# Kept merge weights, a ring that grows from 10 to 12 slots, later output sums and early norms in a streaming encoder with gathered experts

## What is computed

```python
def layer(x, ...):
    h = rmsnorm(x, norm1_g)
    z = h @ w_in                      # three mixers' inputs and three gates per channel
    ...                               # A: gated linear recurrence, B: pooling, C: differential attention
    g = sigmoid(gates).reshape(B, T, 3, D_MODEL)
    m = g[:, :, 0] * (ya @ proj_a) + g[:, :, 1] * (yb @ proj_b) + g[:, :, 2] * (yc @ proj_c)
    x = x + m @ w_out
    x = x + peer(rmsnorm(x, norm2_g), peer_wq, peer_subkeys, peer_u, peer_v)

def peer(h, wq, subkeys, u, v):
    q = (h @ wq).reshape(n, 8, 2, 128)
    s = einsum('nhpd,pkd->nhpk', q, subkeys)
    top_s, top_i = top_k(s, 16)                       # per half of the key
    best_s, best_c = top_k(all sums of the two halves, 16)
    idx, gate = i1 * 128 + i2, softmax(best_s)        # 8 heads x 16 experts for each token
    act = gelu(einsum('nd,nhkd->nhk', h, u[idx]))
    return einsum('nhk,nhkd->nd', gate * act, v[idx])
```

## Time and profile before

| | us |
|---|---|
| median of 3 runs (2737.83 to 2743.10) | 2740.68 |
| the profiled execution | 2747.89 |
| its span in the profile | 2746.2 |
| layer 0: mixers, experts | 24 to 407, 407 to 1374 |
| layer 1: mixers, experts | 1390 to 1767, 1767 to 2728 |

### The profile page before, as it was taken

One profiled execution on the slowest core, in us unless ns is written; L12 is line 12 of the kernel. 1 busy time (PEld: TensorE's weight loads), 2 busy tenths in 40 slices (PEclk: granted clock), 3 DMA queues, 4 the chain that ended last, 5 costly groups with the idle time before them and its releaser, 6 DMA issues.

```text
span 2746.2 us, 37846 instructions
## 1 busy us (share of the span) xinstructions
PE 2055.8 (75%) x11668; PEld 1180.6 (43%) x11668; DVE 1591.9 (58%) x4244; ACT 699.0 (25%) x1688; POOL 776.8 (28%) x831
## 2 busy tenths in 40 slices
PE   6999988887777665555689999888877775665555
PEld 4566776664343211111256667756643441111111
DVE  2544236564667777777535341455646677777774
ACT  3422213331312222112233221133313132212112
POOL 0122003332343344443201220132313434334431
PEclk9999999998898788888899999999988988788887
DMA  6134559998899999999842347599989999999996
GB/s 198 33 96 154 206 199 418 417 418 345 352 420 411 391 390 389 385 397 387 326 121 60 95 146 259 215 417 417 418 326 370 416 407 375 391 393 387 393 389 241
DMA packets 209345, 862.93 MB, mean 314 GB/s; under 512 B 20144, under 2 KB 91328, under 8 KB 127232
## 3 DMA queue, kind: packets, MB, share of 16 engines
q0 software_dynamic: 95280, 677.21, 60.7%
q1 hardware_dynamic: 113872, 183.38, 19.0%
HBM read 853.82 MB, written 6.71 MB: 313 GB/s over the span
## 4 chain that ended last, share of the span: by engine, by line
DMA 28%; PE 28%; DVE 13%; issue 12%; PEldq 7%; PEld 4%; DVEq 3%; ACT 2%; POOL 2%; ACTq 0%; POOLq 0%; SPq 0%
DMA MIX_RINGS<-in_peer_uv_dram,IDX 23%; PE ps L699 9%; PEldq L922 7%; PE ps L936 4%; DVE MIX_RINGS L1474 3%; DMA W<-in_peer_uv_dram,IDX 3%; PE ps L711 3%; DVEq L1322 3%; PE ps L789 2%; PEld ps L920 2%; PE ps L920 2%; PEld ps L761 2%; PE ps L745 1%; PE ps L727 1%; ACT GC L1131 1%
## 5 line engine op out<-in xcount | busy, mean ns | idle before, releaser
L920 PE MATMUL ps<-MIX_RINGS,GC 64*64 64x512 f32 x4272 | 685.0, 713 | 337.9 <-ACT GC L1131 298.2
L646 POOL DMA_INDIRECT MIX_RINGS<-in_peer_uv_dram,IDX x448 | 484.8, 1082 | 1019.6 <-PEq L922 657.7
L920 PEld LDWEIGHTS ps<-MIX_RINGS,GC 64*64 64x64 f32 x4272 | 199.3, 156 | 701.4 <-issue 701.2
L1474 DVE CUSTOM_DVE_ANT_0 MIX_RINGS<-MIX_RINGS 128x1024 f32<-128x1024 f32 x270 | 324.5, 1224 | 139.5 <-DMA MIX_RINGS<-in_peer_uv_dram,IDX 129.7
L1131 ACT ACTIVATE GC<-twins,WV 128x64 f32<-128x64 f32 x640 | 170.7, 336 | 637.2 <-DVEq L1487 636.6
L1474 DVE CUSTOM_DVE_ANT_0 MIX_RINGS<-MIX_RINGS,WQKV_E 128x1024 f32<-128x1024 f32 x178 | 215.0, 1225 | 152.8 <-DMA MIX_RINGS<-in_peer_uv_dram,IDX 146.0
L920 PE MATMUL ps<-W,GC 64*64 64x512 f32 x1248 | 180.5, 708 | 108.2 <-ACT GC L1131 93.8
L699 PE MATMUL ps<-WQKV_E,HT 128*128 128x384 f32 x768 | 252.8, 486 | 0.7 <-issue 0.7
L920 PE MATMUL ps<-WQKV_E,GC 64*64 64x512 f32 x624 | 151.6, 706 | 98.9 <-ACT GC L1131 85.2
L1126 ACT ACTIVATE GV<-AV 128x4 f32<-128x4 f32 x160 | 32.9, 205 | 703.7 <-DVEq L1475 703.6
L646 POOL DMA_INDIRECT W<-in_peer_uv_dram,IDX x128 | 136.3, 1065 | 242.4 <-PEq L922 214.9
(11 more groups left out here) (255 smaller groups left out, 2808.0 us busy)
## 6 DMA issues: line engine op xcount, KB each, us to landing
W<-in_merge_w_dram SPq DMA_DIRECT2D x40, 1024.0 KB, 4.9
W<-in_merge_w_dram SPq DMA_DIRECT2D x80, 512.0 KB, 9.6
WQKV_E<-in_w_in_dram SPq DMA_DIRECT2D x48, 512.0 KB, 6.6
W<-in_out_w_dram SPq DMA_DIRECT2D x16, 1024.0 KB, 10.5
W<-in_query_w_dram SPq DMA_DIRECT2D x16, 1024.0 KB, 11.2
W<-in_w_in_dram SPq DMA_DIRECT2D x12, 1024.0 KB, 8.2
W<-in_query_w_dram SPq DMA_DIRECT2D x20, 512.0 KB, 10.6
MIX_RINGS<-in_peer_uv_dram,IDX POOLq DMA_INDIRECT x448, 11.1
```

The source lines that it names most:

```text
L646: pool.indirect_dma_start(UV[p % RING], None, table, bass.IndirectOffsetOnAxis(IDX[:, n % 2, j:j + 1], 0))\
L920: pe.matmul(ps[o:o + CHUNK, n:n + 512], w[r, :], v[r, d * 512:(d + 1) * 512], start=False, stop=False, skip_group_check=True)
L1474: dve.tensor_tensor_reduce(u, u, HN[t], 1.0, 0.0, ALU.mult, ALU.add, AV[:, j:j + 1])
```

## The change

The change has these parts:

- **Kept weights.** `KEPT = 2`: the weights of the last merge unit of tile 0 (column blocks 6 and 7) stay in W and serve the chunks 0 to 3, `BLOCK_OF` maps chunks to column blocks. `out_w` for `first_output` goes to four other areas (`OUTW`) and the chunks 4 to 15 load their halves, 30 instead of 40. A chunk's weights are issued behind the query half of the step.
- **Ring.** `JOIN` gives the pick from which a slot takes part. There are ten slots from the first pick, of which the last two (W[2], W[4]) wait until chunk 3 is done, and two more: W[3] from pick 84 (step 21), W[1] from pick 160 (step 40). Each pick takes the slot used longest ago.
- **Output sums.** DVE adds output sum u in step u + 16 instead of u + 15. Norm 2 of tiles 1 and 2 moves from step 19 to 20, the rest queries from 21 to 22. The route of unit 8 is spread differently over the parts, and the clearing for tile 2 comes one step later.
- **Early norms.** All gain rows come in one tensor `gains`. The first is loaded right behind the input, that of the next layer (or the final one) within the expert phase. Norm 1 of the next layer for tile 0 is computed by DVE in step 35, for tile 1 in step 79 between dots and weigh; PE turns tile 0 at step 78 and tile 1 behind the last step. At the boundary only tile 2 is left. Only unit 0 of `w_in` is loaded before the boundary, and units 1 to 5 behind the small loads (`FF_SLOT`).
- **Order on PE.** chunk(s+3) goes ahead of experts(s). The gates of chunk 0 go ahead of the turn of norm 2 for tile 0. On DVE the clearing of tile 0's sums goes behind the first route.

```diff
+JOIN = [0] * 10 + [84, 160]
+SLOT_OF, PREV, NTH = [], [], []
+for _p in range(PICKS):
+    _last = [max([q for q in range(_p) if SLOT_OF[q] == r], default=r - len(JOIN)) if JOIN[r] <= _p else PICKS
+             for r in range(len(JOIN))]
+    _r = _last.index(min(_last))
...
-FF_SLOT = (2, 0, 1, 3, 4, 2)
+FF_SLOT = (0, 2, 3, 4, 1, 0)
...
+KEPT = 2
+BLOCK_OF = [KC - KEPT + i if i < KEPT else i - KEPT for i in range(KC)]
...
-Q_STEP = OUT_STEP + GB + 3
+TURN_STEP = OUT_STEP + GB + 2
+Q_STEP = TURN_STEP + 2
...
-        WH = [W2[i // 2][:, i % 2] for i in range(6)]
+        WH = [W2[i][:, k] for i in (0, 1, 3) for k in range(2)]
...
-        UV = [MIX[:, i, :] for i in range(1, 5)] + [W[:, i].rearrange("p c n -> p (c n)") for i in (3, 4)]\
-            + [UVX] + [MIX[:, i, :] for i in (5, 6, 7)]
+        WF = [W[:, i].rearrange("p c n -> p (c n)") for i in range(SLOTS)]
+        UV = [MIX[:, i, :] for i in range(1, 5)] + [UVX] + [MIX[:, i, :] for i in (5, 6, 7)] + [WF[i] for i in (2, 4, 3, 1)]
+        OUTW = [two(x).rearrange("p k (c n) -> p k c n", c=KC) for x in (MIX[:, 1, :], MIX[:, 2, :], UVX, MIX[:, 0, :])]
...
+            sp.dma_start(G, bcast(gains[0])).then_inc(gain_in.sem, 16)
             sp.wait_ge(setup.sem, 8)
...
-                for u in range(3):
-                    ff_unit(u)
-
+                ff_unit(0)
                 sp.wait_ge(*layer_done.at(l, 0))
-                sp.dma_start(G, bcast(norm1_g[l])).then_inc(gain_in.sem, 16)
...
-                for u in range(3, 3 * HB):
+                for u in range(1, 3 * HB):
                     ff_unit(u)
...
                 def chunk_weights(c):
+                    dc = c // 2
                     for i in CHUNK_W[c % 2]:
-                        if c < 2:
-                            sp.wait_ge(*w_used[i // 2].at(l, BEFORE_REST[i // 2]))
+                        if dc == KEPT:
+                            sp.wait_ge(*half_used[(0, 0, 1, 1, 3)[i]].at(l, 1 + (0, 1, 0, 1, 0)[i]))
                         else:
-                            sp.wait_ge(*half_used[i].at(l, c // 2))
+                            sp.wait_ge(*half_used[i].at(l, dc))
...
-                for c in range(AHEAD):
-                    chunk_weights(c)
                 for s in range(4 * (PH - AHEAD)):
-                    if s + AHEAD < CHUNKS:
-                        chunk_weights(s + AHEAD)
                     if s % 4 < 2:
                         query_half(s // 4 * 2 + s % 4)
+                    if 2 * KEPT <= s + AHEAD + 1 < CHUNKS:
+                        chunk_weights(s + AHEAD + 1)
...
+                sp.wait_ge(*gain_used.at(l, 2))
                 sp.nop(nofuse=True)
-            sp.wait_ge(*layer_done.at(DEPTH, 0))
-            sp.dma_start(G, bcast(final_g)).then_inc(gain_in.sem, 16)
+                sp.dma_start(G, gains[bass.ds(l * 2 + 2, 1)].rearrange("a d -> (a d)").partition_broadcast(P))\
+                    .then_inc(gain_in.sem, 16)
...
-                    if RING - AHEAD <= p < RING:
-                        pool.wait_ge(*pq_ps.at(l, p - (RING - AHEAD) + 1))
-                    pool.wait_ge(*uv_free.at(l, p + 1 - RING))
+                    r = SLOT_OF[p]
+                    if NTH[p] == 0:
+                        if r in (5, 6, 7):
+                            pool.wait_ge(*pq_ps.at(l, r - 4))
+                        if r in (8, 9):
+                            pool.wait_ge(*cb_ps.at(l, 2 * KEPT))
+                        if r == 10:
+                            pool.wait_ge(*half_used[4].at(l, KC))
+                            pool.nop(nofuse=True)
+                            pool.wait_ge(*wqh_used.at(l, 2 * (PH - AHEAD)))
+                        if r == 11:
+                            pool.wait_ge(*w_used[1].at(l, SLOT_USES[1]))
+                    else:
+                        pool.wait_ge(*uv_free.at(l, PREV[p] + 1))
...
+            norm_turn(0, 0, range(2))
             with pe.Fori(0, DEPTH) as l:
-                norm_turn(l, 0, range(TILES))
+                norm_turn(l, 0, [2])
...
+                chunk(l, 0, [0])
                 norm_turn(l, 1, [0])
...
-                chunk(l, 0)
+                chunk(l, 0, [1])
...
-                    experts(l, s)
                     if s + AHEAD < CHUNKS:
                         chunk(l, s + AHEAD)
+                    experts(l, s)
...
-                    if s == OUT_STEP + GB + 1:
+                    if s == TURN_STEP:
                         norm_turn(l, 1, [1, 2])
...
+                    if s == GROUPS - 2:
+                        pe.wait_ge(*x_done.at(l, 2))
+                        norm_turn(l + 1, 0, [0])
+                norm_turn(l + 1, 0, [1])
...
+                    if s == GROUPS - 1:
+                        turned(l + 1, 0, range(2))
...
-                clear(0)
                 route(l, 0, range(4))
+                dve.wait_ge(*nt_ev.at(l, (TILES + 1) * TURNS))
+                dve.nop(nofuse=True)
+                clear(0)
...
-                    if 0 <= s - OUT_STEP - 1 < GB:
-                        rest_output(l, s - OUT_STEP - 1)
-                    if s == OUT_STEP + GB + 1:
+                    if 0 <= s - OUT_STEP - 2 < GB:
+                        rest_output(l, s - OUT_STEP - 2)
+                    if s == TURN_STEP:
                         normed(l, 1, 1)
                         normed(l, 1, 2)
+                        dve.drain().then_inc(gain_used.sem, 1)
+                    if s == BEGIN_T[1] + 3:
+                        normed(l + 1, 0, 0)
+                    if s == GROUPS - 1:
+                        normed(l + 1, 0, 1)
...
-                        route(l, n + 2, range(g * k, (g + 1) * k))
+                        late = (0, 0, 2, 3, 4) if n + 2 == PH else range(0, 5 * k, k)
+                        route(l, n + 2, range(late[g], late[g + 1]))
                     weigh(l, t, g, s)
```

More of the change, by code:

```diff
@@ L78 @@
 BEGIN_T = [min(s for s, (n, _) in enumerate(STEPS) if ORDER[n][0] == t) for t in range(TILES)]
-RING_USES = [(PICKS - r + RING - 1) // RING for r in range(RING)]
+JOIN = [0] * 10 + [84, 160]
[4 more added lines that the diff above has]
+    _r = _last.index(min(_last))
+    PREV.append(max(_last[_r], -1))
+    NTH.append(SLOT_OF.count(_r))
+    SLOT_OF.append(_r)
+RING_USES = [SLOT_OF.count(r) for r in range(len(JOIN))]
 N_DG = 8
@@ L169, in build, with two @@
         G = GC[:, 0:D_MODEL]
+        def two(a):
+            return a.rearrange("p (k n) -> p k n", k=2)
         cut = parts("YT_SALL", 16 * TOK)
@@ L358, in build @@
         m0_ev = signal("m0_ev", GB, start=1)
+        outw_in = [landing(f"outw_in{i}", 1) for i in range(GB)]
         mta_ps = signal("mta_ps", GB)
@@ L362, in build @@
         xa_ev = signal("xa_ev", GB)
-        half_in = [landing(f"half_in{i}", KC) for i in range(5)]
+        half_in = [landing(f"half_in{i}", KC - KEPT) for i in range(5)]
         half_used = [signal(f"half_used{i}", KC) for i in range(5)]
@@ L381, in build @@
         idx_ready = signal("idx_ready", UNITS)
-        uv_in = [landing(f"uv_in{i}", RING_USES[i]) for i in range(RING)]
-        uv_free = signal("uv_free", PICKS, start=RING)
+        uv_in = [landing(f"uv_in{i}", RING_USES[i]) for i in range(len(JOIN))]
+        uv_free = signal("uv_free", PICKS)
         av_ready = signal("av_ready", GROUPS)
@@ L391, in build @@
         stored = landing("stored", 0)
-        def two(a):
-            return a.rearrange("p (k n) -> p k n", k=2)
         def bcast(row):
@@ L524, in _ @@
                 sp.nop(nofuse=True)
+                for u in range(GB):
+                    sp.dma_start(OUTW[u].rearrange("p k c n -> p k (c n)"),
+                                 out_w[l, 2 * u:2 * u + 2].rearrange("k p m -> p k m")).then_inc(outw_in[u].sem, 16)
                 for h in range(AHEAD):
@@ L744, in first_output @@
                 for c in cs:
-                    i = pe.matmul(two(bank(n, 0, UNIT)), MT0[:, c, :], W2[n][:, :, c, :],
+                    i = pe.matmul(two(bank(n, 0, UNIT)), MT0[:, c, :], OUTW[n][:, :, c, :],
                                   start=c == 0, stop=c == KC - 1, skip_group_check=True)
@@ L748, in first_output, with chunk, weights, product @@
                     i.then_inc(xa_ps.sem, 1)
-                    pe.drain().then_inc(w_used[n].sem, 1)
-            def chunk(l, c):
+            def chunk(l, c, parts=(0, 1)):
                 dc = c // 2
-                if c >= 2:
-                    pe.wait_ge(*sb_ev.at(l, c - 1))
-                    pe.wait_ge(*mb_ev.at(l, c - 1))
-                def product(to, i, rows, moving):
+                def weights(i):
+                    if dc < KEPT:
+                        return W2[i][:, dc]
+                    pe.wait_ge(*half_in[i].at(l, dc - KEPT + 1))
+                    return WH[i]
+                def product(to, w, rows, moving):
@@ L779, in chunk @@
-                pe.drain().then_inc(cb_ps.sem, 1)
```

(23 more changed lines are left out.)

93 lines of the change are left out of this document (35 added, 58 removed).

## The result

The changed kernel takes 2640.61 us (median of 4 runs, 2639.16 to 2643.35), the kernel before 2741.89 in the same comparison (2737.83 to 2743.35): a ratio of 0.9634, 95% interval 0.9617 to 0.9651, or 101 us less. The forecast was 2638.

What follows compares the result with a forecast made beforehand. Expert phases were taken as bound by DMA at 418 GB/s plus losses from late gathers. Layer terms of -47 and -42 and edges of -13.7 took the profiled 2747.9 to 2645.1, 2638 us on the median's scale; range 2605 to 2700.

Steps and rivals of the forecast that it cites:

- (a): Expert phase, each layer: ten fewer half-block weight loads, five of them among gathers, -6.3 us (bounds -12.5 to 0).
- (c): First expert steps, each layer: merge chunk ahead of weighted sums on PE delays gathers, +2 us (bounds 0 to +10).
- rival 1: Expert steps: gathers delayed beyond the 7.5 us of DMA queue, chunk fully on the path, 2813 us; 8 in 100.
- (b): Output-sum steps, each layer: DVE's later add ends its wait for PE, -19 us; middle stretch another -2.
- Rival 4: Steps 14 to 17: PE still waits for an add, three banks being too few; hole only halved, +19, 2657 us.
- (d): Late expert steps, each layer: two more ring slots, -18 us (bounds 0 to -30), taken at six tenths.
- (e), the w_in term: Layer 0's expert phase: two units of the next w_in no longer loaded there, -5.0 us.
- (e), the edges: Earlier norms: program start -7.4 us, boundary between layers -1.8 once, program end -4.5; together -13.7.
- End of a layer: Step 79, each layer: tile 1's norm ahead of the last weighing lies on the path, +1.5 us.
- (f): Before the first gathers, each layer: chunk 0's gates fill PE's idle time, gathers start 1.5 us earlier (bounds -3 to +5).

Runs made afterwards that it cites:

- ACT's order: The changed kernel with ACT squaring tile 2 ahead of its copies of turned tiles 0 and 1, and at a layer's end ahead of the jump back: 2628.44 us.

## Why the forecast was right, and where its steps were not

The total was right to 5 us on the profiled pair (2645.1 forecast, 2640.45 measured), by steps of which some were off by more than that and made up for each other: that it came so near is in part luck.

(a) and (c), -4.3 forecast, -2.0 and -0.4 measured. Between the first gather and step 13 of layer 0 the DMA engines moved 82.09 MB before and 80.01 after, at 414 and 408 GB/s:

```profile
DMA packets 14180, 82.09 MB, mean 414 GB/s; under 512 B 1571, under 2 KB 1571, under 8 KB 6767
```

```profile
DMA packets 13631, 80.01 MB, mean 408 GB/s; under 512 B 1506, under 2 KB 1506, under 8 KB 6242
```

2.08 MB at 418 are 5.0 us, not 6.3 (30 half blocks are issued in this stretch and 33 before: three fewer, not five); the lower rate costs 80.01/408 - 80.01/414 = 2.8, not 2. In layer 1 it is 2.43 MB, 5.8 us, against a cost of 5.3 at 403 GB/s. So the bytes were near the forecast, and the cost was larger in layer 1. No run puts the ten half blocks back, so that their bytes brought their full time is argued from these rates alone. The reason given for the cost was half right: the dip is the ring of eight slots. But chunk 3, for which the other two slots wait, is late itself, since PE idles some 5 us in step 0 for DVE's chunk and then runs at a granted clock of 0.77 in layer 0 and 0.64 in layer 1:

```profile
1729.01 5.46 PE L791 MATMUL ps<-HT,W 128*128 128x192 f32 x16 [5.03 <-DVE MIX_RINGS L1559]
```

The same 16 matmuls took 2.84 us in the earlier trace rows. The chunk's place has a sign opposite to the rival's: it saves 13.7 us against the sums first, all in step 0. The point of decision that rival 1 named, the queue of 7.5 us, was not passed: the landing of gathers fell only to 12.9 us median at 420 to 600 us, and the DMA share stayed at 1.02 behind the dip.

(b), -19: -18.2 and -18.1, and the run with earlier sums, in which 18.7 and 16.2 come back, shows that this one line is nearly all of it. Rival 4 (too few banks) did not happen.

(d), -18: -27.7 and -29.8, the step that failed most. The mechanism was right, ten slots too few for the latency. Its size was wrong, by the discount of four tenths for DVE's lumps: the two slots brought 27.1 and 26.3, and with eleven slots DVE does the same work at 410 GB/s. What the earlier trace rows showed, a landing near its lowest, was the better evidence, and DVE's 74% the weaker.

The Trainium skill, page "DMA: Bandwidth & Descriptors", section Specifications, gives about 358 GB/s as the HBM limit of a core, half of a stack's 716 for two cores. The trace of this one core does not agree, with 413 and 416 GB/s over more than 400 us in each layer.

(e), the w_in term of -5.0, isn't seen: steps 36 to 79 gained 27.7 us in layer 0, where two unit loads left, and 29.8 in layer 1, which never had them. With a ring of ten these loads are gone too, and the stretch takes 467.6 us against 468.2 in layer 0. So in a stretch at 387 GB/s the loads had been taking idle DMA time. Whether they would cost their 5.0 us at the 413 GB/s of the longer ring, no run shows.

(e), the edges. Start: -0.2 in place of -7.4. The step that failed is the claim that only the gain held tile 2's norm. I had taken the deviation's time from before, 17.86, but the change itself puts ACT's copies of tiles 0 and 1 ahead of it and of its table loads, which begin 5.1 us later; the moved work's place on ACT's queue was not counted. The other 2.05 us went to PE's slow first unit. The run with ACT's order gives 7.1 us back at the unit's start, and 2.05 in the unit. End of a layer: +2.8 and +2.5 us from gelu 79 to the last add in place of +1.5; the run with the last norm behind shows that it wasn't DVE's norm, and the trace shows PE's chain in its place. Boundary to first unit: -0.8 in place of -1.8, and 1.5 lost again on the slow first unit. End of the program: -4.5, as forecast.

(f), -1.5: -5.0 and -4.4. The sign was right, and that PE would run the queries faster; the size was not. The 22 matmuls of the earlier trace rows were only those up to 393 us, where that view ended. The whole block is

```profile
388.18 6.27 PE L805 MATMUL ps<-HT,MIX_RINGS 128*128 128x128 f32 x32 [0.77 <-ACT HT L1080]
```

and takes 3.84 us after the change. The granted clock was 0.50 from 388.0 to 393.3 us before, and it is 1.00 from 385 to 389 now. In layer 0 that is 2.4 us in the queries and 1.0 from the turn to them (the turn itself takes 1.04 us and not 1.97); the other 1.6 is that the turn begins earlier after PE's second unit. In layer 1 the three are 1.6, 1.0 and 1.9. The forecast had no term for the last, and no run takes the three apart.

Against the forecast's -102.8 the two profiled executions show -108.1. The late stretches brought 19.0 more and the ways from second unit to first gather 6.4; the program's start brought 7.2 less, the first steps of the experts 6.2, the ends of the layers 4.7 and the rest 2.0.

## What to carry to other kernels

Where gathers through a ring land near their shortest time and the DMA engines have gaps, slots are the limit: one more of ten was worth 42 us, and the second 10. A result that is consumed one step after it is made, on an engine that also feeds the maker, closes a loop; one more step between them removed it, and no stage shows a cost of it. When a small step is moved, count its place on every queue it touches, ACT's too: the gain's early load brought 0.2 us of 7.4 until ACT's order was mended, and bytes taken out of a stretch that isn't at its ceiling bring little: 0.6 us here, of 5.0 that they were put at.
